# One visit instead of two between the weight tiles of an HGRN2 head

## The reference, cut to what matters

```python
proj = h @ w_in                       # (B,T,2048) @ (2048, 4*2048)
q, fpre, iv, g = jnp.split(proj, ...)
f = lb + (1.0 - lb) * sigmoid(fpre);  lf = log(f);  k = 1.0 - f
# chunks of 32 tokens, A = cumsum(lf)
s  = einsum('bthc,bjhc,btjhc->btjh', qc, kc, exp(A_t - A_j))
oc = einsum('btjh,bjhv->bthv', s, ic) + einsum('bthc,bhcv->bthv', qc*exp(A), S)
S  = exp(A_last) * S + einsum('bjhc,bjhv->bhcv', kc*exp(A_last - A), ic)
out = (rms_norm(o) * silu(g)) @ w_out
```

## Time and profile before

| what | value |
|---|---|
| median of three runs | 3109.09 us |
| the profiled execution | 3109.92 us |
| its span, first to last instruction | 3108.4 us |
| TensorE busy | 3067.9 us (99% of the span) |
| VectorE busy | 1768.0 us (57%) |
| ScalarE busy | 1161.2 us (37%) |
| granted TensorE clock, mean | 0.996 |
| steady period of one head in `h_in` | 33.71 us |

### The profile page before, as it was taken

How to read it: one execution, slowest core, us unless ns; L and a number is a source line. 1 busy time by engine, 2 the same in 40 slices (tenths; PEclk the granted TensorE clock), 3 DMA queues, 4 the chain that set the end, 5 groups by cost and what they waited for, 6 DMA issues and landing times.

```text
span 3108.4 us, 58044 instructions
## 1 busy us (share of the span) xinstructions
PE 3067.9 (99%) x23167; PEld 3027.4 (97%) x23167; DVE 1768.0 (57%) x3168; ACT 1161.2 (37%) x1754; POOL 74.6 (2%) x132
## 2 busy tenths in 40 slices
PE   8999999999999999999999999999999999999998
PEld 7999999999999999999999999999999999999998
DVE  6556565555445544555678788775554445544554
ACT  4333334333223322334445555544333233322333
POOL 2000000000000000000000000000000000000000
PEclk9999999999999999999999999999999999999999
DMA  6565655555555555555555555555555555555543
GB/s 161 149 192 141 194 152 157 150 148 149 149 149 149 148 149 149 149 142 142 152 151 157 162 151 164 160 142 155 150 148 149 150 148 148 150 152 147 148 135 114
DMA packets 855607, 470.25 MB, mean 151 GB/s; under 512 B 10488, under 2 KB 845184, under 8 KB 855520
## 3 DMA queue, kind: packets, MB, share of 16 engines
q1 hardware_dynamic: 843120, 433.09, 50.7%
q0 software_dynamic: 10144, 35.74, 3.8%
q10 hardware_dynamic: 2256, 0.19, 0.1%
HBM read 447.46 MB, written 21.53 MB: 151 GB/s over the span
## 4 chain that ended last, share of the span: by engine, by line
PE 97%; DVE 1%; ACT 1%; issue 0%; DMA 0%; DVEq 0%; SPq 0%; ACTq 0%
PE bank L444 31%; PE bank L445 30%; PE bank L446 30%; PE bank L1886 1%; DVE w_lo L434 0%; PE bank L1933 0%; DMA arena<-in_x_sample_dram 0%; PE bank L1762 0%; PE bank L1918 0%; PE bank L1721 0%; PE bank L1752 0%; PE bank L1931 0%; PE bank L1783 0%; ACT w_hi L427 0%; PE bank L1828 0%
## 5 line engine op out<-in xcount | busy, mean ns | idle before, releaser
L444 PE MATMUL bank<-h_hi,w_hi 128*128 128x320 f32 x4608 | 1434.4, 311 | 5.1 <-issue 2.6
L445 PE MATMUL bank<-h_lo,w_hi 128*128 128x320 f32 x4608 | 1425.9, 309 | 0.0
L446 PE MATMUL bank<-h_hi,w_lo 128*128 128x320 f32 x4608 | 1425.8, 309 | 0.0
L427 ACT ACTIVATE w_hi<-raw 128x1024 fp32r<-128x1024 f32 (+3 forms) x840 | 820.9, 1025 | 839.5 <-PE bank L446 839.3
L434 DVE TENSOR_TENSOR w_lo<-raw,w_hi 128x1024 fp32r<-128x1024 f32 (+3 forms) x840 | 964.4, 1189 | 215.0 <-ACT w_hi L427 213.3
L444 PEld LDWEIGHTS bank<-h_hi,w_hi 128*128 128x128 f32 x4608 | 867.2, 188 | 17.1 <-issue 13.3
L445 PEld LDWEIGHTS bank<-h_lo,w_hi 128*128 128x128 f32 x4608 | 867.4, 188 | 3.0 <-issue 2.8
L446 PEld LDWEIGHTS bank<-h_hi,w_lo 128*128 128x128 f32 x4608 | 867.1, 188 | 0.0
L444 PE MATMUL bank<-g_hi,w_hi 128*128 128x320 f32 x1904 | 590.9, 310 | 3.3 <-DVE w_lo L434 3.2
L446 PE MATMUL bank<-g_hi,w_lo 128*128 128x320 f32 x1904 | 588.3, 309 | 0.0
L445 PE MATMUL bank<-g_lo,w_hi 128*128 128x320 f32 x1904 | 588.3, 309 | 0.0
(11 more groups left out here) (324 smaller groups left out, 1427.2 us busy)
## 6 DMA issues: line engine op xcount, KB each, us to landing
raw<-in_ffn_w_up_dram SPq DMA_DIRECT2D x176, 1024.0 KB, 5.8
raw<-in_ffn_w_down_dram SPq DMA_DIRECT2D x64, 1024.0 KB, 5.8
raw<-in_hgrn_w_in_dram SPq DMA_DIRECT2D x64, 1024.0 KB, 6.6
raw<-in_mlstm_w_in_dram SPq DMA_DIRECT2D x48, 1024.0 KB, 5.9
raw<-in_ffn_w_down_dram SPq DMA_DIRECT2D x32, 768.0 KB, 4.8
raw<-in_mlstm_w_out_dram SPq DMA_DIRECT2D x12, 1024.0 KB, 5.8
raw<-in_hgrn_w_out_dram SPq DMA_DIRECT2D x12, 1024.0 KB, 5.8
raw<-in_state_mlstm_C_dram POOLq DMA_DIRECT2D x8, 1024.0 KB, 6.2
```

The source lines that it names most:

```text
L427: act.activation(w_hi[:, s % 2, part], raw[:, ph.slot(s), part], ACT.Copy).then_inc(hi_done, 1)
L444: pe.matmul(out, tile_hi, hi[:, k, :], start=(k == 0), stop=False)
L445: pe.matmul(out, tile_hi, lo[:, k, :], start=False, stop=False)
L446: last = pe.matmul(out, tile_lo, hi[:, k, :], start=False, stop=(k == ph.blocks(s) - 1))
```

## The change

`h8(two_back)` and `turn_values(one_back)` move on TensorE from behind tile 0 to behind tile 1, directly ahead of `by_columns(one_back)`. On ScalarE `h6(one_back)` moves behind `split_high` of tile 2 and `h2`. On VectorE `h9(two_back)` moves behind `split_low` of tile 2. The waits inside each function stay as they are; `h7` stays behind tile 2.

```diff
 # ScalarE, h_body
                 else:
                     h5(one_back)
-                    h6(one_back)
                 split_high(act, H_IN, it, 2)
                 h2(it, one_back)
+                if one_back is not None:
+                    h6(one_back)
                 if two_back is not None:
                     h10(two_back)
 # VectorE, h_body
                 if one_back is not None:
                     h6(one_back)
+                split_low(dve, H_IN, it, 2)
                 if two_back is not None:
                     h9(two_back)
-                split_low(dve, H_IN, it, 2)
                 if one_back is not None:
                     dve.wait_ge(g_levels, one_back + 1)
 # TensorE, h_body
                     norm_pe(pe, 2)
+                products(pe, H_IN, it, 1, h_hi, h_lo)
                 if two_back is not None:
                     h8(two_back)
                 if one_back is not None:
                     turn_values(one_back)
-                products(pe, H_IN, it, 1, h_hi, h_lo)
-                if one_back is not None:
                     by_columns(one_back)
                 products(pe, H_IN, it, 2, h_hi, h_lo)
```

## The result

| | before | after |
|---|---|---|
| median of 16 runs each, side by side | 3110.09 us | 3114.82 us |
| lowest to highest | 3107.22 to 3112.08 | 3111.55 to 3117.97 |
| span of the profiled execution | 3108.4 us | 3113.5 us |
| steady period of a head | 33.71 us | 34.16 us |

The changed kernel takes 4.73 us more; the ratio is 1.0015, with a 95% interval of 1.0008 to 1.0021. So it is slower, by less than the 6.4 us forecast, and its median stands under the line of 0.2% that the forecast used. The interval, 2.5 to 6.5 us, is too wide to tell 4.7 from 6.4.

The account below looks back on a forecast made before the run. TensorE, holding 97% of the chain, was taken as the bound. Waits of 12 x 0.454 + 0.10 + 0.84 = 6.4 us on 3109.09 gave 3115.5 us (+0.206%), own range 3114.3 to 3116.7, wider range 3111.5 to 3118.5.

Parts of the forecast that it names:

- the line of 0.2%: What a measurement can tell from no change, 6.2 us; chances: faster 0.03, within 0.46, slower 0.51.
- The wait on tile 1: TensorE wants tile 1's low part 0.30 us before VectorE has it; with 0.16 restart, 0.45 us a head.
- The idle row: Sign in the new profile: about 0.3 us idle at tile 1's L444, released by VectorE's L434, heads 3 to 14.
- The lateness doesn't heal: VectorE's work from g_o to tile 1's low part is unchanged, so the wait repeats and neither grows nor heals.
- Rival (b): VectorE's 0.57 us gap at the loop's turn halves, leaving the restart alone: +3.0 us, 3112.1 us; chance 0.08.
- Joining saves nothing: Merging TensorE's visit behind tile 0 with by_columns behind tile 1 saves 0.0 us a head, bounds 0 and 0.29.
- Rival (a): A TensorE visit has its own price, so joining two saves 4.4 us: 3111.1 us; chance 0.07.
- rival (c): Faster: VectorE's wait gone and the visit's edges saved too, 3104.7 us; chance 0.03.
- The moved work of the other engines: Moves on ScalarE and VectorE fit before g_levels, with 1.0 and 2.3 us to spare, and cost 0.
- The semaphore's price: From the low half's end to TensorE's weight load: 0.05 us; at 100 ns the sum would be 7.1 us.
- The one-off stalls taken at 0: TensorE's stalls in heads 1 and 2: taken as 0, bounds 0.2 us more, 1.7 us less or more.
- Rival (d): Stray VectorE delays land on TensorE, perhaps with one more lower-clock stretch: 3117.5 to 3119.2 us; chance 0.09.

Follow-up runs that it names:

- the early low part: VectorE's low part of tile 1 moved ahead of h5, in the changed kernel (3109.02 us) and in the kernel before (3108.24 us); ratio 0.9994 each.
- the lists alone: The changed kernel with TensorE's order put back to that of the kernel before, ScalarE's and VectorE's moves kept: 3109.11 us, ratio 0.9996.

## Why the prediction was right, and where it was off

**The wait on tile 1: right.** 0.45 us a head was forecast and 0.45 was measured (34.16 - 33.71), released by L434, in heads 3 to 14. The idle row is 0.17 to 0.20 us and not the 0.3 that was to be looked for: it starts at the modelled end of the matmul before. Head 15 lost 0.61 us instead of 0.84, as its stray delay cost less in this trace. Head 1 shows no wait. Head 2 has no idle row, and its tile 1 starts 0.10 us late, as forecast (1567.91 - 0.147 against 1567.52 + 0.147). Putting the low part earlier removed the wait, and leaving records behind tile 0 removed it by their time.

**The lateness doesn't heal: right.** It is the same in every head from 3 to 14: between `g_o` and the low part VectorE waits for nothing of TensorE's. Rival (b), a shorter gap at the loop's turn, didn't happen: the gap before L1145 is 0.58 us in head 4 (0.57 before), and from the first copy of the outputs at 1624.18 to the low part at 1637.21 it is 13.03 us in both traces. (That head 4 stands at the same absolute times in both is chance.)

**Joining saves nothing: right.** Rival (a) is out by the pair of experiments with the early low part, 33.71 us joint and apart; rival (c), faster, fell with it. The edges belong to the change between the whole array and a quarter of its columns, and cutting the burst in two added exactly one more pair, 0.29 us. By the rule that the forecast cited from the Trainium skill, "TensorEngine Tiling (Array Packing)", Key Properties, a drain where the tiling mode changes, both had to come out so; the runs agree with it (0.00 us from joining, 0.29 us for the added pair).

**The moved work of the other engines: right**, by the experiment with the lists alone, and with the joint visit by the one with the early low part, whose period is 33.71 us too.

**The semaphore's price:** 0.05 us from the end of the low half (1638.43) to the weight load at 1638.48, as in the earlier trace rows, and the same in all 13 heads. The upper end of 100 ns in the Trainium skill, "Advanced Engine Details and Errata", Network/Comms, from which 7.1 us in all was worked out, is not what this case shows.

**The one-off stalls taken at 0: the term that was mis-sized.** It was -1.7 us: one stretch at the lower clock, behind head 2's stall, was spared. The forecast had that as a bound ("1.7 us less or more if one stretch at 1.2 GHz (3.8 x 0.45) goes or comes"). The sum from this trace: 12 x 0.45 + 0.61 + 0.10 - 1.7 = 4.4 us. From head 1's L936 to the last head's the two traces differ by 4.4 us (507.35 and 511.73). Their spans differ by 5.1, so 0.7 us more lies outside this phase, unexplained; the two sets of times differ by 4.7 and 5.9 us. The mis-sized term is read from the traces: the intervals of the times hold 6.4 us as well.

**How near the number came, and what of that is luck.** The difference of 4.7 us is 1.7 us under the forecast and below the forecast's own range of 5.2 to 7.6. The likelier of its two verdicts, slower than the line of 0.2% (0.51), didn't come in the first set: the median ratio is 0.15%, the other verdict (0.46). As an absolute time 3114.82 us is only 0.7 us from the 3115.5 forecast, but that is luck in part: the kernel before had a median of 3110.09 us over 16 runs and not the 3109.09 of the three runs that the forecast started from.

Rival (d), stray delays, is seen in small: one head of 14 in the first trace, two in the second, 0.2 to 0.4 us each. It is in the terms above.

## What to carry to other kernels

Small work between two tiles of a busy TensorE isn't only its own time; it is also the cover under which the next tile's inputs get ready. Before taking it away, compare the end of the producer (here VectorE's low part) with the start that the tile would have then, and add the restart (0.16 us here); if the producer is tied to an earlier point of TensorE's stream, the wait comes back in every round. What costs in a visit is the change of the array's tiling (0.29 us for a pair here), not the visit, so joining two visits of which only one changes the tiling saves nothing.

## What the runs showed of the hardware that was not expected

- Dense small matmuls in code that ran for the first time stalled TensorE here: 288 instructions of `by_columns` used up in about 2 us, then 3.4 and 2.6 us of stall, with a 16 KB packet of instructions landing 1.2 to 1.5 us before each stall's end. With 3.5 us of products put between them both stalls were gone. From head 3 on, the second round of the loop, the same instructions ran without a stall in every trace.
- A stall of 2.4 to 2.9 us in a busy stream was followed by a stretch of 3.4 us at 1.2 GHz, which costs half its length (1.7 us), in three traces of one order of TensorE's work. In five traces of other orders it was not, behind stalls of 2.0 to 2.6 us; with the cut in head 1 alone, a stall of 2.6 us, it came and lasted 6.8 us. What decides is open.
- A VectorE instruction of 0.25 us took 0.6 now and then (0.63 in head 15 of before, 0.58 and 0.63 in heads 8 and 15 of the changed kernel's second trace). In the kernel before this was free, the period staying 33.71 us; in the changed one TensorE paid 0.3 to 0.4 us for it.
